# Two-layer hybrid trunk with grouped experts: the fourth expert's transposed hidden activations in buffers of their own, transposed two weight units earlier on TensorE, and rounded ahead of unit 47

## The reference, cut to what matters

```
scores = sigmoid(t @ router_w);  g_star = group with the best top-2 sum
gates  = the two best experts of g_star, scaled to sum 1, zero elsewhere
for e in range(16):
    y = (silu(t @ w1[e]) * (t @ w3[e])) @ w2[e]      # 1024 -> 512 -> 1024
    out = out + gates[:, e:e+1] * y
x = x + g2 * out
```

## Time and profile before

| | us |
|---|---|
| median of 3 timed runs | 1023.59 (1022.79, 1026.51, 1023.59) |
| the profiled execution, its own time | 1021.63 |
| its span, first to last instruction | 1019.8 |
| PE busy | 949.8 (93% of the span) |
| DVE busy | 756.7 (74%) |
| ACT busy | 611.2 (60%) |
| mean granted TensorE clock | 0.97 |

### The profile page before, as it was taken

One profiled execution on the slowest core, in us unless ns is written; L12 is line 12 of the kernel. 1 busy time (PEld: TensorE's weight loads), 2 busy tenths in 40 slices (PEclk: granted clock), 3 DMA queues, 4 the chain that ended last, 5 costly groups with the idle time before them and its releaser, 6 DMA issues.

```text
span 1019.8 us, 16549 instructions
## 1 busy us (share of the span) xinstructions
PE 949.8 (93%) x5916; PEld 752.4 (74%) x5916; DVE 756.7 (74%) x923; ACT 611.2 (60%) x755; POOL 109.8 (11%) x171
## 2 busy tenths in 40 slices
PE   3799999998999999999996999888999999999996
PEld 0479884587887887878874886577787887888784
DVE  2544258556998988989978533666998989988994
ACT  3533316434878878878755423524888778757782
POOL 5091000001001000000000633010001000001000
PEclk8899999997999999999997999997999999999999
DMA  9997858747999999999986875939999999998971
GB/s 339 363 249 226 291 205 292 267 153 290 366 399 342 398 372 349 394 371 351 392 336 215 260 197 176 341 105 337 394 398 362 396 368 352 392 327 276 349 283 43
DMA packets 146610, 314.03 MB, mean 308 GB/s; under 512 B 13821, under 2 KB 44693, under 8 KB 146530
## 3 DMA queue, kind: packets, MB, share of 16 engines
q1 hardware_dynamic: 135360, 286.53, 78.6%
q0 software_dynamic: 9648, 25.78, 7.5%
q10 hardware_dynamic: 1530, 0.78, 0.3%
HBM read 298.64 MB, written 9.75 MB: 302 GB/s over the span
## 4 chain that ended last, share of the span: by engine, by line
PE 80%; DVE 9%; DMA 5%; ACT 2%; issue 2%; SPq 1%; DVEq 0%; ACTq 0%
PE ps L1745 17%; PE ps L1747 16%; PE ps L1746 16%; PE ps L2250 3%; DMA raw<-in_w_mod 3%; PE ps L1847 2%; DVE wlo L1386 2%; PE ps L1849 2%; PE ps L1848 2%; PE ps L1757 2%; PE ps L2275 2%; DMA raw<-in_moe_w 2%; PE ps L1865 2%; PE ps L2277 2%; PE ps L2276 2%
## 5 line engine op out<-in xcount | busy, mean ns | idle before, releaser
L1386 DVE TENSOR_TENSOR wlo<-raw,whi 128x1024 fp32r<-128x1024 f32 x384 | 453.8, 1219 | 39.9 <-ACT whi L777 38.1
L777 ACT CAST whi<-raw 128x1024 fp32r<-128x1024 f32 x384 | 397.8, 1052 | 108.8 <-PE ps L1747 83.0
L1745 PE MATMUL ps<-whi,xghi 128*128 128x512 f32 x480 | 192.7, 402 | 2.4 <-DVE wlo L1386 2.2
L1747 PE MATMUL ps<-wlo,xghi 128*128 128x512 f32 x480 | 190.3, 396 | 0.0
L1746 PE MATMUL ps<-whi,xglo 128*128 128x512 f32 x480 | 190.1, 396 | 0.0
L1115 DVE TENSOR_TENSOR wlo<-raw,whi 128x1024 fp32r<-128x1024 f32 x56 | 74.5, 1370 | 55.8 <-ACT whi L772 55.8
L1745 PEld LDWEIGHTS ps<-whi,xghi 128*128 128x128 f32 x480 | 90.7, 189 | 25.3 <-DVE wlo L1386 4.4
L1745 PE MATMUL ps<-whi,hidThi 128*128 128x512 f32 x256 | 102.7, 401 | 6.0 <-DVE hidTlo L1456 4.6
L1747 PEld LDWEIGHTS ps<-wlo,xghi 128*128 128x128 f32 x480 | 90.6, 189 | 21.6
L1746 PEld LDWEIGHTS ps<-whi,xglo 128*128 128x128 f32 x480 | 90.7, 189 | 20.3
L1746 PE MATMUL ps<-whi,hidTlo 128*128 128x512 f32 x256 | 101.7, 397 | 0.0
(11 more groups left out here) (328 smaller groups left out, 1407.6 us busy)
## 6 DMA issues: line engine op xcount, KB each, us to landing
raw<-in_moe_w SPq DMA_DIRECT2D x384, 512.0 KB, 6.3
raw<-in_w_mod SPq DMA_DIRECT2D x96, 512.0 KB, 6.2
raw<-in_na_w_in SPq DMA_DIRECT2D x24, 512.0 KB, 10.1
raw<-in_cf_pw_w SPq DMA_DIRECT2D x24, 512.0 KB, 8.1
mods<-mod_scratch POOLq DMA_DIRECT2D x9, 512.0 KB, 6.9
raw<-in_ab_w_out SPq DMA_DIRECT2D x8, 512.0 KB, 5.5
urep<-uT SPq DMA_DIRECT2D x64, 35.5 KB, 2.8
urep<-uT POOLq DMA_DIRECT2D x64, 35.5 KB, 2.4
```

The costliest lines, as they stand in the source:

```text
L777: A.copy(whi[:, (MOE_W[tn.L] + j) % SPL, :], raw[:, (MOE_U[tn.L] + j) % RAW, :]).then_inc(tn.sem("w_rounded"), 1)
L1386: V.tensor_tensor(wlo[:, n % SPL, :], raw[:, (MOE_U[L] + j) % RAW, :], whi[:, n % SPL, :], ALU.subtract).then_inc(tn.sem("unit_done"), 1)
L1745: T.matmul(dst, lhi, rhi, start=first, stop=False)
L1747: return T.matmul(dst, lhi, rlo, start=False, stop=last)
```

## The change

`HID_T[3]` goes from 44 to 42. A new table `HID_ROUND = [18, 26, 38, 47]` says where ACT and DVE take the transposed hidden: as before for experts 0 to 2, and for expert 3 ahead of unit 47 and no longer behind the loop. Since at that time `hidThi` and `hidTlo` are still read by units 42 and 43, expert 3 gets other buffers: `lastThi`/`lastTlo` in the turns, and `wideThi`/`wideTlo` in the wide turn, where the place of the former is taken by `spread_of` (L314) and the place of `xrow` (L327) is free by then. No instruction is added or taken away. What stands at the same place of PE's code, `rows_turned` and `gather`, moves with the transposes.

```diff
@@ -307,6 +307,8 @@
         hid = at("hid", [P, FF], 28)
         hidThi = at("hidThi", [P, FC, P], 30, F32R)
         hidTlo = at("hidTlo", [P, FC, P], 32, F32R)
+        last_hidT = (at("lastThi", [P, FC, P], 46, F32R), at("lastTlo", [P, FC, P], 48, F32R))
+        wide_hidT = (at("wideThi", [P, FC, P], 68, F32R), at("wideTlo", [P, FC, P], 70, F32R))
         yg = at("yg", [P, D], 34)
         yhi = at("yhi", [P, D], 38, F32R)
         ylo = at("ylo", [P, D], 42, F32R)
@@ -480,6 +482,10 @@
 
             return tile[:, n % (RAW if tile is raw else SPL), :].rearrange("p (k n) -> p k n", k=KC // DENSE)
 
+        def hidden_T(tn, e):
+
+            return (hidThi, hidTlo) if e < PER_GROUP - 1 else wide_hidT if tn.after else last_hidT
+
         def moe_slot(tile, n):
             return tile[:, n % (RAW if tile is raw else SPL), :]
 
@@ -926,7 +932,7 @@
 
                 def hidT_round(tn, e):
                     tn.wait(eng, "hid_T", e + 1)
-                    A.copy(hidThi[:], ps[:, BT, :].rearrange("p (k n) -> p k n", k=4)).then_inc(tn.sem("hidT_rounded"), 1)
+                    A.copy(hidden_T(tn, e)[0][:], ps[:, BT, :].rearrange("p (k n) -> p k n", k=4)).then_inc(tn.sem("hidT_rounded"), 1)
 
                 def y_round(tn):
                     tn.wait(eng, "y_scaled", 1)
@@ -954,10 +960,9 @@
                         for e in range(PER_GROUP):
                             if j == W13[e] + 4 + 5:
                                 silu_of(tn, e)
-                            if j == HID_T[e] + 6:
+                            if j == HID_ROUND[e]:
                                 hidT_round(tn, e)
                         round_turn(tn, j)
-                    hidT_round(tn, PER_GROUP - 1)
                     for j in range(W_GROUP, W_GROUP + ahead):
                         round_turn(tn, j)
                     if ahead:
@@ -1453,7 +1457,8 @@
 
                 def hidT_remainder(tn, e):
                     tn.wait(eng, "hidT_rounded", e + 1)
-                    V.tensor_tensor(hidTlo[:], ps[:, BT, :].rearrange("p (k n) -> p k n", k=4), hidThi[:], ALU.subtract) \
+                    hi, lo = hidden_T(tn, e)
+                    V.tensor_tensor(lo[:], ps[:, BT, :].rearrange("p (k n) -> p k n", k=4), hi[:], ALU.subtract) \
                      .then_inc(tn.sem("hidT_rest"), 1)
 
                 def wide_select():
@@ -1503,7 +1508,6 @@
                             for t in range(NT):
                                 link(V.tensor_tensor(xres[:, t, :], xres[:, t, :], yback[:, t, :], ALU.add))
                         rest_turn(tn, j)
-                    hidT_remainder(tn, PER_GROUP - 1)
                     for j in range(W_GROUP, W_GROUP + ahead):
                         rest_turn(tn, j)
                     if ahead:
@@ -2098,7 +2101,7 @@
                                 tn.wait(eng, "hidT_rest", e + 1)
                             for half in range(2):
                                 cut = slice(half * HALF, (half + 1) * HALF)
-                                ins = three(ps[:, BY + half, :], hidThi[:, q, :], hidTlo[:, q, :],
+                                ins = three(ps[:, BY + half, :], hidden_T(tn, e)[0][:, q, :], hidden_T(tn, e)[1][:, q, :],
                                             moe_slot(whi, n)[:, cut], moe_slot(wlo, n)[:, cut],
                                             e == 0 and q == 0, e == PER_GROUP - 1 and q == 3)
                         else:
@@ -2182,7 +2185,7 @@
                                     tn.wait(eng, "y_scaled", min(e, 2))
                             for half in range(2):
                                 cut = slice(half * HALF, (half + 1) * HALF)
-                                ins = three(ps[:, WIDE_BY[e] + half, :], hidThi[:, q, :], hidTlo[:, q, :],
+                                ins = three(ps[:, WIDE_BY[e] + half, :], hidden_T(tn, e)[0][:, q, :], hidden_T(tn, e)[1][:, q, :],
                                             moe_slot(whi, n)[:, cut], moe_slot(wlo, n)[:, cut], q == 0, q == 3)
                         else:
                             if name == "w1" and q == 0 and (e or i):
@@ -2321,7 +2324,8 @@
 
 W13 = [expert_order().index((e, "w1")) * 4 for e in range(PER_GROUP)]
 
-HID_T = [12, 20, 32, 44]
+HID_T = [12, 20, 32, 42]
+HID_ROUND = [18, 26, 38, 47]
 SCATTER = [10, 13, 16, 19]
 
 XG_AT = 2

```

## The result

| | before | changed |
|---|---|---|
| median, us | 1024.35 (4 runs, 1022.79 to 1026.51) | 1015.67 (4 runs, 1015.45 to 1017.46) |
| ratio | | 0.9925, 95% interval 0.9901 to 0.9948 |
| span of the profiled execution | 1019.8 | 1013.7 |

The change saves 8.7 us by the medians, between 5.3 and 10.1 by the interval. The forecast was 8.9. The same code was timed twice more later: 0.9925 (0.9902 to 0.9947) and 0.9916 (0.9893 to 0.9938).

The account below looks back on a forecast made before the run. The prediction took PE to set the pace, with gain only where PE stands still: 4.3 + 3.4 + 1.2 = 8.9 us off 1023.59 gives 1014.7 us, range 1012.3 to 1018.3.

Parts of the forecast that it names:

- The stall with rows: PE's wait between the fourth expert's transposes and unit 44 goes in five turns with rows: 0.86 us each, 4.3 us.
- Without rows: The same wait goes in layer 0's last turn (1.73 us) and the wide turn (1.69 us), together 3.4 us.
- The prepared turn: The 3.74 us gather already stands at that place and PE goes on without idle, so 0 us gained.
- The cover: PE's work from transposes to unit 44, 3.16 us without rows and 4.03 with, hides the 2.09 us chain.
- The wait for hid: Transposes want hid 2.80 us earlier; slack 1.04 us in a looped turn, 0.41 in the wide one; cost 0.
- the slower rival: Late hid stalls the transposes at unit 42; 2.0 us later eats the 8.9 us gain, 3.7 gives 1036.6 us; chance 0.05.
- The bound of 2.2 us for one remainder: If slack before the transposes shrinks by one remainder (1.23 us), PE waits 0.2 us a turn, 0.8 in the wide one.
- ACT's and DVE's orders: The moved cast holds back unit 47's split, which PE needs five units (7.0 us) later; cost 0.
- The loads: Shorter looped turns want 378 GB/s instead of 373; the same loads ran at 396 elsewhere, so no cost.
- the rival: Loads bind anyway and turns stay as they are, 1023.6 us, also the outcome by the 358 GB/s figure; chance 0.08.
- The start of the wide turn: Earlier gather gives DVE a lead, removing 0.3 us at the first product and 0.9 at the third scatter: 1.2 us.
- The clock: A half-clock stretch in the prepared turn, costing 1.7 us, may vanish or double; taken as 0.

Follow-up runs that it names:

- one_unit: Changed kernel with the fourth expert's transposes ahead of unit 43 instead of 42, one unit of cover; ratio 0.9925 to the kernel before.
- late_round: Changed kernel with ACT and DVE taking the fourth expert's transposed hidden behind unit 47, as before the change; ratio 0.9944 to the kernel before, median 1018.27 us.
- hid_late1: Changed kernel with DVE's multiplication for the fourth expert's hid one remainder later, in both of DVE's loops; ratio 0.9971 to the kernel before.
- hid_late2: Changed kernel with DVE's multiplication for the fourth expert's hid two remainders later, in both of DVE's loops; ratio 1.0084 to the kernel before, 1031.15 us.
- xadd_early: Changed kernel with DVE's additions to xres in the wide turn two units earlier in its order; ratio 0.9928 to the kernel before.
- order_only: Changed kernel with the transposes back at unit 44, own buffers and rounding ahead of unit 47 kept; ratio 0.9999 to the kernel before.
- rows_stay: Changed kernel with the next tile's rows and the gather back at unit 44, hidden transposes still ahead of unit 42; ratio 0.9911 to the kernel before, 1014.86 us.
- xadd_hid: xadd_early with the fourth expert's hid also one remainder earlier on DVE in the wide turn; ratio 0.9923 to the kernel before, wide turn 77.93 us.

## Why the prediction was right, step by step

*The stall with rows*, 4.3 us for five turns: 0.86 us a turn forecast, 0.86 measured (0.84 once). *Without rows*, 3.4 us: 1.74 and 1.70 measured. *The prepared turn*, 0: 0.07. Together 7.8 us where 7.7 were forecast. Comparing the place with the same work done without a wait elsewhere in the trace is what made it exact; PE's own idle bracket (0.62 us in the earlier trace rows) would have given 1.2 us too little in five turns.

*The cover*, 3.16 and 4.03 us against a chain of 2.09: it holds in all eight turns, and one_unit and late_round cross it from two sides where the sum says that they should, but for layer 0's last turn in late_round.

*The wait for hid*, costed at 0 with a slack of 1.04 and 0.41 us: 0 in the changed kernel, and the slack is real, as hid_late1, hid_late2 and xadd_early show. But the prediction gave layer 0's last turn the 1.04 us of a looped one, and it has 0.3. Two remainders delay `hid` by 2.80 us in a looped turn (ready 4.57 us after unit 40's first product, was 1.77); the formula of the slower rival gives 14.7 us of waiting for that, and the turns lost 13.9 us between units 41 and 45. Its turning point was put at 2.0 us, where the formula gives 8.3 us; it takes 2.1 to eat 8.9. The bound of 2.2 us for one remainder was too small, it cost about 4.4 by the turns, 1.18 of them in layer 0's last one.

*ACT's and DVE's orders*, costed at 0: order_only shows it, 0.9999.

One sign was off: the cast was to wait some 1.5 us for the transposes and waits 0.79, since ACT ends unit 46's cast just ahead of them.

*The loads*, costed at 0: from 386 to 456 us no load is waited for, at 375 GB/s. In the first turn of each layer ACT waits 14 and 16 times for one (3 and 18 times before), which is one of the prediction's signs of being wrong, but the place at the fourth expert gained its 0.86 us in them all the same. The figure of 358 GB/s, which the prediction set against this, was half a reading of the Trainium skill. In HBM Reference, section Specifications, it is a core's share when both cores of a domain stream; the same section says that a core streaming alone measures about 425 GB/s. Here one core runs, so the 373 to 396 GB/s of the rows agree with the section, and the outcome ascribed to it in the rival is not what it says.

*The start of the wide turn*, 1.2 us: this step was too large. The lead came (5.6 us, forecast 5.9) and took the 0.3 us at the first product. Of the 0.9 us at the third scatter only 0.2 came. Between the two, DVE has to wait for the next expert's rows, which PE turns at the fourth unit and ACT rounds:

```profile
929.34 1.29 DVE L1521 TENSOR_TENSOR xg2lo<-ps,xg2hi 128x512 fp32r<-128x512 f32 x2 [1.15 <-ACT xg2hi L974]
```

DVE idles 1.15 us there and 0.17 and 0.15 us at two other places. In the kernel before and in rows_stay it doesn't idle once on this way. So of the 2.0 us won at the first unit only 0.3 reach the addition. It was wrong to let a lead at the turn's start stand for a lead 17 units later. What holds the scatter is the place of the addition in DVE's order, as xadd_early shows, and what holds the turn is that DVE is full: rid of one wait, PE came to the next.

*The clock*, 0 with 1.7 us either way: the half-clock stretch of the prepared turn was in both profiles, so it changed nothing here. Its price is nearer 1.5 us (below).

Sum by the turns: 7.8 us at the fourth expert and 0.5 in the wide turn, 8.3 us where 8.9 was forecast. The medians say 8.7. That they come within 0.2 us of the forecast is partly luck: the term of the wide turn was too large by 0.7 us, and the interval of the medians is wider than that on both sides.

## What to carry to other kernels

Where one engine is busy without a break, look for the place at which it waits for a chain through two others, and put work of its own between: here two units of 1.4 us hid a chain of 2.1 us, and moving the other engines' part alone did nothing. Price such a stall by the same work done elsewhere without it. And ask what the moved step waits for in its turn: an engine in order made 1 us of slack into the next stall as soon as something was put ahead of it, and what was won in one place of a turn with a second full engine came back as a wait in another. Read that slack in every turn: the smallest, 0.3 us, was in one that had been counted with the others.

## What the runs showed of the hardware

In the prepared turn a half-clock stretch may or may not fall behind the single-column products. Two profiles, of the changed kernel and of one_unit, whose prepared turns are alike up to there:

```profile
903.00:918.00 15.00, 15.00 (x89) 13.21 (x89) 9.73 (x13) 6.27 (x8) 0.97 (x1) 0.89 0.97 337
```

```profile
903.00:918.00 15.00, 15.00 (x96) 13.34 (x96) 10.54 (x13) 7.05 (x10) 0.97 (x1) 1.00 0.95 335
```

PEclk is 0.89 and 1.00, and the prepared turn takes 78.24 and 76.67 us: such a stretch costs about 1.5 us. It was there in the three profiles of the changed kernel and not in those of one_unit, xadd_early and xadd_hid. The last two have no edit but in the wide turn, which comes after, so it isn't the edit that decides it; from the runs I can't say what does. And the first product behind a group of transposes costs 0.08 us more than the pitch each time: a unit takes 1.47 us there instead of 1.40, at the full clock, in every turn of every kernel where that unit has no wait in it.
